# A streaming encoder on one core: the first layer's input and the memory are loaded a second time, already turned, and normalised in that form

## What is computed

```
h  = rmsnorm(x, g_norm[l])            # x * rsqrt(mean(x*x) + eps) * gain, per token
P  = h @ w_in[l]                      # queries, keys, values and gates of branches A, B, C, M
mk, mv = rmsnorm(mem, g_mem[l]) @ w_mem_kv[l]      # 256 memory tokens
o_A = top-k sparse attention, chosen by an indexer;  o_B = forgetting attention
o_C = chunk-band attention;           o_M = cross-attention into the memory
x  = x + concat(o * silu(gate)) @ w_out[l]
```

## Time and profile before

| | |
|---|---|
| time, median of 3 runs | 1713.91 us (1713.59 to 1715.81) |
| the profiled execution, its own time | 1712.33 us |
| its span, first to last instruction | 1710.5 us |
| PE busy | 1692.7 us, 99% of the span |
| DVE / ACT / POOL busy | 59% / 39% / 14% |
| data moved | 166.64 MB, mean 97 GB/s |
| in the first of 40 slices (about 43 us) | 285 GB/s, DMA engines 80% busy |

### The profile page before, as it was taken

The page is one execution under the profiler, slowest core; times in us unless marked ns, Lnnn a source line. Parts: engine busy times, 40 slices in busy tenths (PEclk is TensorE's granted clock), DMA queues, the critical chain, the costliest instruction groups (busy, mean ns, idle before and its releaser), DMA issues.

```text
span 1710.5 us, 30251 instructions
## 1 busy us (share of the span) xinstructions
PE 1692.7 (99%) x10866; PEld 1103.7 (65%) x10866; DVE 1005.7 (59%) x2707; ACT 662.3 (39%) x1599; POOL 239.7 (14%) x452
## 2 busy tenths in 40 slices
PE   9999999999999999999999999999999999999998
PEld 4466677767778755555444677767777886555553
DVE  3645888778878333333235378887888772333321
ACT  4532334333343345454124323343333433445531
POOL 1233321100010010002012433220000001000000
PEclk9999999999999999999999999999999999999999
DMA  8344322223132322114421533231231324221130
GB/s 285 94 143 126 127 94 87 97 78 106 41 134 94 103 79 97 40 47 115 129 94 51 166 104 127 94 137 44 81 109 38 132 97 121 69 90 37 46 108 37
DMA packets 60340, 166.64 MB, mean 97 GB/s; under 512 B 11345, under 2 KB 29745, under 8 KB 57889
## 3 DMA queue, kind: packets, MB, share of 16 engines
q1 hardware_dynamic: 43584, 125.88, 23.0%
q0 software_dynamic: 16608, 38.83, 6.9%
HBM read 137.03 MB, written 30.73 MB: 98 GB/s over the span
## 4 chain that ended last, share of the span: by engine, by line
PE 80%; DVE 14%; DMA 2%; issue 2%; ACT 1%; DVEq 1%; ACTq 0%; SPq 0%
PE psX L876 54%; DVE lower L1268 9%; PE psT L816 7%; PE psX L1052 6%; PE psS L985 6%; DVE work L1490 2%; PE psS L904 2%; DMA wring<-in_w 2%; PE psS L816 1%; PE psX L816 1%; PE psX L1027 1%; DVE gate L1322 0%; PE psS L954 0%; PE psS L924 0%; DVE sc L1434 0%
## 5 line engine op out<-in xcount | busy, mean ns | idle before, releaser
L876 PE MATMUL psX<-wring,hT 128*128 128x512 f32 (+2 forms) x2016 | 834.3, 557 | 6.4 <-ACT kv L1146 3.0
L876 PEld LDWEIGHTS psX<-wring,hT 128*128 128x128 f32 x2016 | 363.9, 190 | 327.5 <-issue 318.6
L1268 DVE TENSOR_SCALAR_CACHE_REDUCE lower<-sc,thr 128x640 uint8<-128x640 f32 (+5 forms) x462 | 407.3, 934 | 17.5 <-issue 9.5
L876 PE MATMUL psX<-hT,wring 128*128 128x128 f32 x2880 | 334.6, 275 | 0.9 <-ACT gate L1166 0.4
L876 PEld LDWEIGHTS psX<-hT,wring 128*128 128x128 f32 x2880 | 327.7, 192 | 3.6 <-issue 3.0
L1208 ACT ACTIVATE work<-work,stat 128x256 f32<-128x256 f32 (+7 forms) x288 | 200.0, 694 | 295.9 <-DVEq L1493 293.3
L1217 ACT COPY work<-psT 128x512 f32<-128x512 f32 (+2 forms) x352 | 156.7, 488 | 321.0 <-PE psT L816 319.7
L816 PEld LDWEIGHTS psT<-con,work 128*128 128x128 f32 x1080 | 121.4, 141 | 73.2 <-issue 66.5
L816 PE MATMUL psT<-con,work 128*128 128x128 f32 x1080 | 158.2, 278 | 0.0
L1490 DVE CUSTOM_DVE_ANT_0 work<-psS,bias 128x640 f32<-128x640 f32 (+7 forms) x120 | 86.2, 718 | 41.9 <-issue 20.5
L1490 DVE CUSTOM_DVE_ANT_0 work<-psS,sc 128x384 f32<-128x384 f32 (+5 forms) x48 | 42.8, 891 | 72.1 <-PE psT L816 70.0
(11 more groups left out here) (203 smaller groups left out, 1537.9 us busy)
## 6 DMA issues: line engine op xcount, KB each, us to landing
wring<-in_w SPq DMA_DIRECT2D x17, 2048.0 KB, 9.4
cache<-in_kB SPq DMA_DIRECT2D x16, 512.0 KB, 7.0
cache<-in_vB SPq DMA_DIRECT2D x16, 512.0 KB, 4.1
cache<-in_kC SPq DMA_DIRECT2D x16, 512.0 KB, 6.8
cache<-in_vC SPq DMA_DIRECT2D x16, 512.0 KB, 4.7
scratch_oscr<-gate POOLq DMA_DIRECT2D x54, 128.0 KB, 2.0
hT<-scratch_oscr SPq DMA_DIRECT2D x18, 384.0 KB, 3.6
kv<-in_x SPq DMA_DIRECT2D x9, 512.0 KB, 5.7
```

The source lines that it names most:

```text
L876: mm = pe.matmul(out, lhs, rhs, start=(kt == 0), stop=(kt == KT - 1))
L1268: v.tensor_scalar(lower[:, at:at + STRIP_L[t]], sc[:, o], thr[:, n:n + 1], 0.0, ALU.is_lt, ALU.add, accum_out=below[:, n:n + 1])
```

## The change

The host hands the input and the memory over twice: as rows (`x`, `mem`) and turned (`xT`, `memT`). The rows are still loaded and squared. In `comes_turned` tiles (first layer's 0 to 8, and the memory's 9 and 10 in both layers) the turned copy is loaded straight into `hT` or `memT`; DVE multiplies it by the gain, which is now a column per channel in the constants (C_GT), as soon as it has landed; DVE takes the reciprocal as before; PE does one transpose of the reciprocal broadcast over 128 columns, which leaves in `psS` the 128 reciprocals along the row on every partition; and DVE multiplies the turned tile by that. ACT's copy is gone for these tiles. The gain loads of the first layer and of the memory (L744, L748, each broadcast to 128 partitions) are gone.

```diff
+TURNED_IN = {"x0": range(0, 1), "x1": range(1, 2), "x2": range(2, 3), "x3": range(3, 5), "x5": range(5, 9), "m": range(9, 11)}
+def comes_turned(l, n):
+    return l == 0 or n > ST_
@@ program_order
     emit("X", ("x", 0))
     emit("ident")
-    emit("gn")
+    emit("XT", "x0")
     emit("head")
     emit("X", ("x", 1))
+    emit("XT", "x1")
     emit("W", "A1")
+    emit("gm")
     emit("con")
     emit("X", ("x", 2))
+    emit("XT", "x2")
     emit("X", ("x", 3))
-    emit("gm")
+    emit("XT", "x3")
+    emit("XT", "x5")
     emit("W", "mm")
+    emit("XT", "m")
     emit("norm", 0)
@@ with_loads
-        gone = (l, ("turn", t)) if kind != "r" else (l + 1, ("turn" if l + 1 < DEPTH else "y", t))
+        gone = (l, ("norm", t)) if kind != "r" else (l + 1, ("turn" if l + 1 < DEPTH else "y", t))
...
             put(at[(l, ("P", "A1", 0))], l, "gm")
+            put(at[(l, ("P", "A1", 0))], l, "XT", "m")
@@ SP, step X: what a slot's next tile waits for
-                            sp.wait_ge(*S.fill(("turn", pt), pl).on(("turn", pt), pl))
+                            sp.wait_ge(*squares.on(pt, pl))
@@ SP, new step XT
+                    if s[1] == "m":
+                        src = d["memT"].rearrange("p (k c) -> p k c", k=KT)
+                        sp.dma_start(memT[:, :, :], src).then_inc(xT_loaded["m"].sem, 16)
+                    else:
+                        cols = slice(group[0] * P, (group[-1] + 1) * P)
+                        src = d["xT"].rearrange("p (k c) -> p k c", k=KT)
+                        sp.dma_start(hT[:, :, cols], src[:, :, cols]).then_inc(xT_loaded[s[1]].sem, 16)
@@ PE, step turn
+                    if comes_turned(l, n):
+                        turn(S.ap(s)[:, 0:P], rstd[:, 2, n:n + 1].to_broadcast([P, P])).then_inc(S.fill(s).sem, 1)
+                        continue
@@ DVE, step norm
+                    if comes_turned(l, n):
+                        dve.wait_ge(*xT_loaded[x].on(x))
+                        c0 = C_GT + KT * (l + 1 if n > ST_ else 0)
+                        v.tensor_tensor(turned_tile(n), turned_tile(n), con[:, c0:c0 + KT].unsqueeze(2).to_broadcast([P, KT, P]),
+                                        ALU.mult)
+                        dve.wait_ge(*rooted.on(n))
+                        v.reciprocal(rstd[:, 2, n:n + 1], rstd[:, 1, n:n + 1]).then_inc(normed.sem, 1)
+                        dve.drain()
+                        continue
@@ DVE, step turn
+                    if comes_turned(l, n):
+                        roots = S.ap(s)[:, 0:P].unsqueeze(1).to_broadcast([P, KT, P])
+                        v.tensor_tensor(turned_tile(n), turned_tile(n), roots, ALU.mult).then_inc(S.empty(s).sem, 1)
```

More of the change, by code:

```diff
@@ L516, in encoder @@
         gateA = bias[:, 0:(NT + 1) * W].rearrange("p (t c) -> p t c", c=W)
-        gmem = bias[:, 0:D]
         dec = [bias[:, 0:2 * SEQ].rearrange("p (h c) -> p h c", h=2), xr[:, :, :]]
@@ L601, in encoder @@
         outs = [(l, s[1:]) for l, s in steps("P") if s[1][0] == "O"]
-        gain_loaded = Signal(sem("gain_loaded"), [(l, "g") for l in range(DEPTH + 1)], lambda e: 16)
-        small_loaded = Signal(sem("small_loaded"), [(l, "g") for l in range(DEPTH)], lambda e: 32)
+        gain_loaded = Signal(sem("gain_loaded"), [(l + 1, "g") for l in range(DEPTH)], lambda e: 16)
+        small_loaded = Signal(sem("small_loaded"), [(l, "g") for l in range(DEPTH)], lambda e: 16)
+        xT_loaded = {x: Signal(sem(f"turned_{x}_loaded"), [(l, x) for l in range(DEPTH) if not l or x == "m"], lambda e: 16)
+                     for x in TURNED_IN}
         squares = Signal(sem("squares_summed"), norms)
@@ L609, in encoder @@
         half_loaded = Signal(sem("half_of_b1_loaded"), [(l, "B1") for l in range(DEPTH)], lambda e: 16)
-        h_act = Signal(sem("hT_by_act"), events(["turn"], lambda s: s[1]))
+        h_act = Signal(sem("hT_by_act"), [(l, s[1]) for l, s in steps("turn") if not comes_turned(l, s[1])])
         h_dve = Signal(sem("hT_by_dve"), events(["turn"], lambda s: s[1]))
@@ L694, in merged, with turned_tile @@
             return gate[:, t, first * P:(first + n) * P].rearrange("p (g c) -> p g c", g=n)
+        def turned_tile(n, first=0):
+            if n > ST_:
+                return memT[:, first:, (n - 9) * P:(n - 8) * P]
+            return hT[:, first:, n * P:(n + 1) * P]
         def tile_of(l, n):
@@ L743, in _ @@
                             sp.wait_ge(*o_stored[t].on("M", l - 1))
-                    sp.dma_start(gain, d["gain"][2 * l:2 * l + 1, :].to_broadcast([P, D])).then_inc(gain_loaded.sem, 16)
+                    sp.dma_start(gain, d["gain"][l - 1:l, :].to_broadcast([P, D])).then_inc(gain_loaded.sem, 16)
                 elif k == "gm":
@@ L820, in scores_free @@
                 old = S.prior(use)
-                if old and old[1][0] == "turn":
+                if old and old[1][0] == "turn" and not comes_turned(old[0], old[1][1]):
                     pe.wait_ge(*h_act.on(old[1][1], old[0]))
@@ L849, in _ @@
                         if c in ("A1", "mm"):
-                            pe.wait_ge(*h_act.on(t + (9 if c == "mm" else 0)))
-                            pe.wait_ge(*h_dve.on(t + (9 if c == "mm" else 0)))
+                            n = t + (9 if c == "mm" else 0)
+                            if not comes_turned(l, n):
+                                pe.wait_ge(*h_act.on(n))
+                            pe.wait_ge(*h_dve.on(n))
                         if c == "O0":
@@ L1096, in _ @@
                                          scale=1.0 / D, bias=con[:, C_EPS:C_EPS + 1]).then_inc(rooted.sem, 1)
-                elif k == "turn":
+                elif k == "turn" and not comes_turned(l, s[1]):
                     n = s[1]
@@ L1100, in _ @@
                     src = S.ap(s)[:, 0:4 * P].rearrange("p (b c) -> p b c", b=4)
[L1101 to L1105, removed]
+                    nc.scalar.copy(hT[:, 0:4, n * P:(n + 1) * P], src)
                     act.drain().then_inc(h_act.sem, 1)
@@ L1276, in _ @@
                     n = s[1]
+                    if comes_turned(l, n):
+                        x = [x for x in TURNED_IN if n in TURNED_IN[x]][0]
+                        if n == 0:
+                            dve.wait_ge(s_ident, 16)
+                        dve.wait_ge(*xT_loaded[x].on(x))
[6 more added lines that the diff above has]
+                        continue
                     dve.wait_ge(*rooted.on(n))
@@ L1288, in _ @@
                     v.scalar_tensor_tensor(out=src, in0=src, scalar=rstd[:, 2, n:n + 1],
-                                           in1=gain if n <= ST_ else gmem, op0=ALU.mult, op1=ALU.mult).then_inc(normed.sem, 1)
+                                           in1=gain, op0=ALU.mult, op1=ALU.mult).then_inc(normed.sem, 1)
                 elif k == "turn":
@@ L1832, in lay_out @@
     con, tmask = constants()
+    by_channel = lambda rows: a(rows.T.reshape(KT, P, -1).transpose(1, 0, 2).reshape(P, -1))
+    con[:, C_GT:C_GT + 3 * KT] = by_channel(np.stack([g_norm[0], g_mem[0], g_mem[1]]).astype(np.float32)
+                                            ).reshape(P, KT, 3).transpose(0, 2, 1).reshape(P, -1)
+    x = a(np.concatenate([x_prompt.reshape(SEQ, D), x_sample.reshape(P, D)]))
+    mem = a(mem_prompt.reshape(MEM, D))
     return {
-        "x": a(np.concatenate([x_prompt.reshape(SEQ, D), x_sample.reshape(P, D)])),
-        "mem": a(mem_prompt.reshape(MEM, D)),
+        "x": x, "xT": by_channel(x), "mem": mem, "memT": by_channel(mem),
         "w": a(w.reshape(-1, KT * 512)),
-        "gain": a(np.concatenate([np.stack([g_norm, g_mem], 1).reshape(2 * DEPTH, D), g_final[None]])),
+        "gain": a(np.concatenate([g_norm[1:], g_final[None]])),
         "bf": a(b_f),
```

18 lines of the change are left out of this document (8 added, 10 removed).

## The result

The changed kernel takes 1716.19 us, median of 20 runs (1715.02 to 1718.07); beside it on the same chip the kernel before took 1713.73 us (20 runs, 1712.39 to 1716.84). The ratio is 1.0014, interval 1.0007 to 1.0020: slower by 0.14%, less than the 0.2% that counts as a change. Forecast were 1716.8 us and 0.17%. The profiled execution took 1716.64 us, its span is 1714.9.

The account below looks back on a forecast made before the run. PE was taken as the bound, busy 1692.7 of 1710.5 us. Net +1.7 plus 1.2 for the clock, over the profiled 1712.33, gave 1715.2; the median lies 1.6 above: 1716.8 us, with 8 in 10 from 1711.5 to 1719.8.

Parts of the forecast that it names:

- PE's saving: PE's queue, 13 turns: one transpose (0.11 us) for eight (0.87), 0.76 us saved each, 9.9 us if nothing takes it back.
- DVE's multiplication: DVE's part of a turn: 1,024 columns with one operand in psS, 1.225 us, 0.53 more than the copy it replaces.
- the rival at half speed: DVE reads the repeated operand at half speed: 1.2 us more in nine turns behind tile 4, about 1727 us; chance 2%.
- The waits behind tiles 8 to 10: PE waits for the psS buffer ahead of the indexer's matmuls: 0.4, 0.75 and 0.75 us, together 1.9 us.
- The queue: SP's loads: 14.2 us more ahead of input tile 4, landing at 40.4, needed by 34.7; its turn starts 6.6 us later.
- tile 4 is in time: Rival at input tile 4's load: it lands by 34.7 us, the sum is -4.0 us, giving 1709.9 us; chance 10%.
- The clock: TensorE's clock behind the 5.7 us stop before tile 4's turn: costs between nothing and 2.6 us, taken as 1.2.
- the clock falls in full: Rival: the clock falls in full while PE waits for tile 4, costing 2.6 us, 1718.2 us; chance 20%.
- The weights: A1 weights' second part, behind turned tiles 0 and 1: 2.4 us later, PE waiting until 15.9 instead of 13.57.
- only tile 4's landing counts: Before tile 4's turn: the stop swallows the weights' 2.4 us and the saving of turns 0 to 3.
- off PE's path: The gain's multiplication on DVE and ACT's lost copies, in the second layer too: counted as nothing.
- The sum: Whole kernel: +6.6 at tile 4's turn, 3.4 back in turns 4 to 10, 1.5 in the second layer: net +1.7 us.

Follow-up runs that it names:

- the second profile of before: The kernel before, unchanged, executed once more for a second profile: 1715.29 us; every turn from tile 1 to tile 10 stands 1.6 us later than in its first profile.
- the first experiment: The changed kernel with the turned tiles 5 to 8, the memory's weights and the turned memory issued behind input tile 4: 1711.24 us, ratio 0.9977 to the kernel before.
- the one with more bytes: The kernel before with 5.8 MB of weight loads that nothing reads issued ahead of input tile 4: 1724.74 us, ratio 1.0055.

## Why the prediction was right

Point by point, in its own order.

*PE's saving* was 0.76 us a turn: the single transpose takes 0.11 in every timeline above, and tile 2 to tile 3 takes 6.78 us instead of 7.43. That is 0.65 less, so 0.11 of the 0.76 was lost. The forecast allowed a wait of 0.3 there.

*DVE's multiplication* took 1.22 us (forecast 1.225). The repeated operand costs nothing, and the rival at half speed is out.

*The waits behind tiles 8 to 10* were put at 0.4, 0.75 and 0.75. PE waited 0.4 and 0.7 behind tiles 8 and 9; from tile 10 to the next mark 11.52 us passed instead of 11.70, so 0.58 of its saving was lost. With that the turns 4 to 10 gave back 3.5 us (forecast 3.4): +7.4 at turn 4, +2.5 by the clock, +6.4 when the weights are issued. In the second layer the lag falls from 4.3 us (880.68 against 876.34 at its turn of the tile before the memory) to 2.8 (944.26 against 941.44): 1.5, as forecast, and as much between the two second profiles.

*The queue.* Tile 4 landed at 41.0 (forecast 40.4) and its turn began at 45.5 (44.8), +7.4 us instead of +6.6. The terms of the sum hold one by one: from one landing to the next passed 1.7 us for turned tile 2, 2.9 for the pair, 5.5 for tiles 5 to 8 and 2.8 for the turned memory, where 1.82, 3.15, 5.6 and 2.6 were taken. The agreement of the whole is closer than its ground: from the second profile of before (tile 4 at 27.9) the same sum gives 42.1, against 41.0 and, in the changed kernel's second profile, 41.6. The Trainium skill's 512 B for line rate (DMA: Bandwidth & Descriptors, Specifications) would have had it land at 37.8, or at 39.5 from the second profile; the landings lie nearer to the measured 288 GB/s on either base. The rival "tile 4 is in time" did not happen, but the first experiment shows its mechanism: worked out were 4.0 us less than before, measured 3.9 by the ratio of 0.9977 and 3.3 by the medians. That the size agrees so well is in part luck: turn 4 stood 3.1 us behind the second profile of before and not 0.9, and what came behind it gave back 7.2 us and not 4.9.

*The clock* is a term that was mis-sized: 1.2 us were taken, half way between 0 and 2.6, and the two traces show 2.5 and 1.3. What the rival "the clock falls in full" has for a condition came true in both traces, and by the mean clocks in most runs; the first trace shows its whole price, the second half of it. The fall to 0.50 agrees with what the Trainium skill says of a wait between bursts (TensorE: Matmul & The Clock Gate, HAM oscillation).

*The weights* are another term that was off, without effect: PE resumed at 16.8, not 15.9, and then ran at half speed until about 20 (3.6 us to the turn of tile 1, where 2.3 were taken). Both vanish in the stop before tile 4, as the forecast said of everything ahead of it: "only tile 4's landing counts". In the kernels that load tile 4 ahead this cover is gone: there the weights ahead of tile 1 brought its turn 1.6 us forward. That the weights were late at all comes from the early base: the forecast's 2.4 us on top of the 15.1 of the second profile of before give 17.5, and the changed kernel's two profiles have 16.8 and 17.2.

*A term that the sum had at nothing:* the first layer behind tile 10. From the issue of weights at 288.41 to that at 584.50 pass 296.1 us in both executions of before (295.4 in the one with more bytes), and 295.0 in all nine of kernels with turned tiles. In that stretch PE's waits for ACT and DVE fall from 1.8 to 0.8 us. The forecast had the lighter work of these two "off PE's path"; that it is what shortens these waits is likely, but no run shows it by itself.

*The sum.* The profile of before that it was made against began 1.6 us early, and the 1.6 us by which the median lay above that execution were added at the end; these took care of each other. Net of that, +7.4 - 3.5 - 1.5 + 2.5 = +4.9 by the first trace (span +4.4), and +6.3 - 3.5 - 1.5 + 1.3 = +2.6 from the two second ones, whose spans however differ by -0.1 us. The medians say +2.5 and +3.2. So the mechanism is shown, and the sign; that the forecast lay within 0.6 us of the median is luck in part, since its terms were off by about 1 us each in both directions, and single executions differ by more.

What stays open: how much of the clock's cost reaches the medians, and what makes the steps between executions. Behind tile 10 the nine executions with turned tiles part in three stretches, from about 120 to 290, 865 to 945 and 965 to 1,140 us, by up to 4.0, 2.5 and 1.9 us, and no single row carries it.

## What to carry to other kernels

Work that goes off the bounding engine into a load pays only if the load does not stand ahead of another that is needed sooner: on one queue, add up the bytes at the rate of their piece size, and put next to each load the moment at which it is needed. Look for the consumer that waits in line on an engine with unrelated work behind it; here ACT's square of a tile held up the copy for one two tiles older, so that a load was due 4.4 us before its own use. A stop of the matmul engine of several us has a second price, the clock behind it.

## What the runs showed of the hardware

- SP is held when turned tiles (512 B to 2 KB pieces) are outstanding: single issues took 5.92, 2.98 and 2.88 us, and tile 4 was issued at 24.07 instead of 9.58. In the three executions without turned tiles no single issue of the first 45 us took more than 1.60 us, not even with 5.8 MB of long rows in the queue. It did not make tile 4 later by itself: the computation from bytes alone gave its landing within 0.6 us from one profile of before and 1.1 from the other.
- The granted clock fell to 0.50 behind stops of 4.8, 6.3 and 9.1 us, and stayed at 1.00 with most of the stop filled (2.2 us left). The longer stop cost less: 1.3 us lost behind 6.3 us, 2.5 behind 4.8. In both the clock was at 0.50 for 6.8 us, but from 43.9 to 50.7 in the one and from 41.9 to 48.7 in the other, where the stop itself covered more than 3 us of it and not 1; behind the stop of 9.1 us 1.7 us were lost. The last two rows of stretches above give the way back: 0.50 until 50 us, 0.83 in the next two.
- In the first 20 us PE's slow stretch lies at another place in each execution, and here it began at waits of only 3.5 and 2.7 us. In the changed kernel's first profile it is from 16.8 to 20:

```profile
14.00:16.00 2.00, 0.00 (x0) 0.00 (x0) 1.03 (x2) 0.00 (x0) 0.00 (x0) 1.00 0.50 186
16.00:18.00 2.00, 1.19 (x2) 0.77 (x3) 0.00 (x0) 0.00 (x0) 0.00 (x0) 0.64 0.98 398
18.00:20.00 2.00, 2.00 (x4) 0.76 (x4) 0.00 (x0) 0.00 (x0) 0.00 (x0) 0.51 1.10 347
```

in its second one from 11.2 to about 16: six matmuls take 4.23 us there, and the next six, from 17.25, take 2.56.

```profile
11.19 4.23 PE L914 MATMUL psX<-wring,hT 128*128 128x456 f32 x6 [2.66 <-DMA wring<-in_w]
17.25 2.56 PE L914 MATMUL psX<-wring,hT 128*128 128x456 f32 x6 [1.83 <-DMA wring<-in_w]
```
